# Second layer's mixing output taken tile by tile: first column chunk's halves in buffers of their own, the two chunks' order changed, the second tile's norm moved

## The reference, cut to what matters

```python
o = merge_branches(y_ml, y_ga, y_na, zg, w_branch[l], w_out[l])      # ... @ w_out
x = x + ga1 * rms_norm_2(o, g_post_mix[l])
f = conv_ffn(modulate(rms_norm_2(x, g_pre_ffn[l]), sh2, sc2), w_up[l], conv_w[l], conv_b[l], w_down[l])
x = x + ga2 * rms_norm_2(f, g_post_ffn[l])
```

## Time and profile before

| | |
|---|---|
| median of three runs | 1708.37 us |
| the profiled execution, its own time | 1708.59 us |
| its span in the profile | 1706.8 us |
| PE busy | 1670.8 us, 98% of the span |
| DVE busy | 1257.1 us, 74% |
| ACT busy | 842.5 us, 49% |

### The profile page before, as it was taken

One profiled execution on the slowest core, in us unless ns is written; L12 is line 12 of the kernel. 1 busy time (PEld: TensorE's weight loads), 2 busy tenths in 40 slices (PEclk: granted clock), 3 DMA queues, 4 the chain that ended last, 5 costly groups with the idle time before them and its releaser, 6 DMA issues.

```text
span 1706.8 us, 25221 instructions
## 1 busy us (share of the span) xinstructions
PE 1670.8 (98%) x9808; PEld 1426.8 (84%) x9808; DVE 1257.1 (74%) x2205; ACT 842.5 (49%) x1370; POOL 0.2 (0%) x4
## 2 busy tenths in 40 slices
PE   9989999999999999999999999999999999999998
PEld 9888888777787778888888888889778989979987
DVE  7999777875778798856877775347756786678864
ACT  6665555554334444347444442336553455466653
POOL 0000000000000000000000000000000000000000
PEclk9999999999999999999999999999999999999999
DMA  8646542231234335533545556324222444547553
GB/s 342 225 161 237 192 151 96 78 124 63 64 117 161 121 133 185 200 134 99 139 146 188 194 196 222 99 74 139 99 84 63 135 146 152 177 151 176 188 186 135
DMA packets 79078, 254.91 MB, mean 149 GB/s; under 512 B 14320, under 2 KB 18672, under 8 KB 78320
## 3 DMA queue, kind: packets, MB, share of 16 engines
q1 hardware_dynamic: 73488, 244.91, 42.9%
q10 hardware_dynamic: 5472, 8.39, 1.4%
HBM read 252.19 MB, written 1.07 MB: 148 GB/s over the span
## 4 chain that ended last, share of the span: by engine, by line
PE 76%; DVE 15%; ACT 5%; issue 3%; DMA 0%; ACTq 0%; SPq 0%; DVEq 0%
PE bank L725 64%; DVE w_lo L1828 4%; PE bank L868 2%; PE bank L1037 2%; PE bank L1023 2%; PE bank L1115 2%; PE bank L1014 2%; ACT w_hi L1225 1%; DVE mod_w L1885 1%; DVE probT L1885 1%; PE bank L1104 1%; DVE att L2455 1%; DVE xc L1928 1%; DVE resid_x L2321 0%; DVE bank L2453 0%
## 5 line engine op out<-in xcount | busy, mean ns | idle before, releaser
L1828 DVE TENSOR_TENSOR w_lo<-w_raw,w_hi 128x1024 fp32r<-128x1024 f32 (+1 forms) x356 | 427.2, 1211 | 253.8 <-ACT w_hi L1225 252.3
L1225 ACT ACTIVATE w_hi<-w_raw 128x1024 fp32r<-128x1024 f32 (+1 forms) x356 | 370.1, 1048 | 338.7 <-PE bank L725 284.8
L725 PE MATMUL bank<-hT_hi,w_hi 128*128 128x512 f32 (+1 forms) x1280 | 446.2, 349 | 1.7 <-ACT zo L1553 0.6
L725 PE MATMUL bank<-hT_hi,w_lo 128*128 128x512 f32 (+1 forms) x1280 | 437.8, 342 | 0.0
L725 PE MATMUL bank<-hT_lo,w_hi 128*128 128x512 f32 (+1 forms) x1280 | 437.6, 342 | 0.0
L725 PEld LDWEIGHTS bank<-hT_hi,w_hi 128*128 128x128 f32 x1280 | 241.7, 189 | 30.1 <-issue 3.1
L725 PEld LDWEIGHTS bank<-hT_hi,w_lo 128*128 128x128 f32 x1280 | 241.6, 189 | 28.0
L725 PEld LDWEIGHTS bank<-hT_lo,w_hi 128*128 128x128 f32 x1280 | 241.9, 189 | 27.1 <-issue 1.0
L1885 DVE SCALAR_TENSOR_TENSOR mod_w<-mod_w,c_rows 128x1024 f32<-128x1024 f32 x96 | 117.1, 1220 | 7.8 <-DMA mod_w<-in_mod_weights 7.8
L725 PE MATMUL bank<-w_hi,hT_hi 128*128 128x512 f32 x272 | 114.8, 422 | 0.4 <-issue 0.4
L725 PE MATMUL bank<-w_lo,hT_hi 128*128 128x512 f32 x272 | 106.6, 392 | 0.0
(11 more groups left out here) (393 smaller groups left out, 2796.8 us busy)
## 6 DMA issues: line engine op xcount, KB each, us to landing
w_raw<-in_weights SPq DMA_DIRECT2D x356, 512.0 KB, 4.0
mod_w<-in_mod_weights SPq DMA_DIRECT2D x96, 512.0 KB, 4.1
nbias<-in_window_bias ACTq DMA_DIRECT2D x32, 128.0 KB, 3.0
resid_c<-in_ctx ACTq DMA_DIRECT2D x2, 1024.0 KB, 6.1
gain_mix<-gain_rows SPq DMA_DIRECT2D x3, 512.0 KB, 5.6
gain_ffn<-gain_rows SPq DMA_DIRECT2D x3, 512.0 KB, 4.3
c_rows<-in_conditions SPq DMA_DIRECT2D x1, 1024.0 KB, 5.5
gatew<-in_gate_weights SPq DMA_DIRECT2D x1, 1024.0 KB, 11.5
```

The lines of the kernel that those rows point to most:

```text
L725: mm = pe.matmul(held[key][:, oc], st, mv_, start=(opens and k == 0 and t == 0 and i == 0), stop=(closes and k == tiles - 1 and t == 2), s ...
L1225: a.activation(w_hi[:, p % RING, :, used], w_raw[:, p % RING, :].rearrange("p (k n) -> p k n", k=KP)[:, :, used], ACT.Copy).then_inc(hi_re ...
L1828: v.tensor_tensor(w_lo[:, p % RING, :, used], w_raw[:, p % RING, :].rearrange("p (k n) -> p k n", k=KP)[:, :, used], w_hi[:, p % RING, :, ...
```

## The change

In the last layer only:

- The halves of A0 to A3 get places of their own (`hold_hi`, `hold_lo`), so their splits wait for no earlier piece; the waits of B0 to B3 and U0 to U3 on `piece_used` are renumbered to match.
- PE takes the mixing product in the order: A for tile 2, B for tile 2, B for tile 3, A for tile 3. The pieces of B are released by B for tile 3. `norm_T` of tile 2 stands behind the first piece of A for tile 3.
- `norm_T` of tile 3 stands behind the whole of tile 2's part of the first `w_up` chunk.
- ACT and DVE have programs of their own for this stage (`output_apart`, `post_apart`), with a small extra square root ahead of the first real one.

```diff
+HELD = stream().index(("w_out_2", LAYERS - 1, 0, 0))
...
+    hold_hi = sb("hold_hi", [P, RING, KP, COLS], R + 32 * KB, F32R)
+    hold_lo = [sb(f"hold_lo{i}", [P, 2, KP, COLS], (16 + 16 * i) * KB, F32R) for i in range(2)]
...
+    def used_before(p):
+        if HELD <= p < HELD + RING:
+            return 0
+        if HELD + RING <= p < HELD + 2 * RING:
+            return p - 2 * RING + 1
+        if HELD + 2 * RING <= p < HELD + 3 * RING:
+            return p - 2 * RING + 1
+        return p - RING + 1
...
+                turn_at = n if l == LAYERS - 1 and which == "ffn" else n - 1 if shared(l, which) or late else n // 2
...
-                        if gi == 0 and p == (n - 1 if shared(l, which) or late else n // 2):
+                        if gi == 0 and p == turn_at:
                             norm_T(l, which, 1)
...
+                    if gi == 0 and turn_at == n:
+                        norm_T(l, which, 1)
...
+                def out_apart():
+                    at = pieces[0]
+                    for c, t in ((0, 2), (1, 2), (1, 3), (0, 3)):
+                        key = (("wo", l, c), t - NT)
+                        ps = take(pe, key)
+                        for p in range(RING):
+                            i = at + RING * c + p
+                            if t == NT:
+                                pieces[0] = i + 1
+                                pe.wait_ge(hi_ready, i + 1)
+                                pe.wait_ge(lo_ready, i + 1)
+                                if c == 0:
+                                    pe.wait_ge(*merged_ready.at((l, KP * p + KP - 1)))
...
+                            if t > NT:
+                                mm.then_inc(piece_used, 1)
+                            if t > NT and c == 0 and p == 0:
+                                norm_T(l, "ffn", 0)
...
-                    if p >= RING:
-                        act.wait_ge(piece_used, p - RING + 1)
+                    if used_before(p) > 0:
+                        act.wait_ge(piece_used, used_before(p))
...
+            def output_apart(l):
...
+                split_hi(up)
+                act.wait_ge(*merged_ready.at((l, KD - 1)))
+                copied(0, 2, False)
+                a.activation(rs[:, 60:61], eps[:], ACT.Sqrt).then_inc(*A.next())
+                squared(1, 2, True)
+                rooted(2)
+                norm_root(*nxt, 2, o_of("mix", 2))
+                split_hi(up + 2)
+                copied(1, 3, False)
+                norm_hi(*nxt, 0, 0)
+                split_hi(up + 3)
+                norm_hi(*nxt, 0, 1)
+                split_hi(up + 4)
+                norm_hi(*nxt, 0, 2)
+                norm_hi(*nxt, 0, 3)
+                squared(0, 3, True)
+                rooted(3)
+                norm_root(*nxt, 3, o_of("mix", 3))
+                for p in range(KD // 2):
+                    norm_hi(*nxt, 1, p)
...
+            def post_apart(l, gains):
...
+                split_lo(up)
...
+                norm_gains(*nxt)
+                post_gains(*nxt)
+                gained(0, 2)
+                residual(1, 2)
+                norm_right(*nxt, 2)
+                split_lo(up + 2)
+                gained(1, 3)
+                norm_tmp(*nxt, 0, 0)
+                split_lo(up + 3)
+                norm_lo(*nxt, 0, 0)
+                norm_tmp(*nxt, 0, 1)
+                split_lo(up + 4)
+                norm_lo(*nxt, 0, 1)
+                norm_tmp(*nxt, 0, 2)
+                norm_lo(*nxt, 0, 2)
+                norm_tmp(*nxt, 0, 3)
+                norm_lo(*nxt, 0, 3)
+                residual(0, 3)
+                norm_right(*nxt, 3)
+                norm_second(*nxt)
```

More of the change, by code:

```diff
@@ L1170, in _ @@
                 merge(2)
-                for c in range(2):
+                def out_apart():
[11 more added lines that the diff above has]
+                                    pe.wait_ge(*merged_ready.at((l, KP * p + KP - 1)))
+                            hi, lo = halves_of(i)
+                            for kk in range(KP):
+                                k = KP * p + kk
+                                for j, (w, x) in enumerate(((hi, mg_hi), (hi, mg_lo), (lo, mg_hi))):
+                                    mm = pe.matmul(ps[:], tokens(x, k, slice(t * P, (t + 1) * P)), w[:, kk, :],
+                                                   start=(k == 0 and j == 0), stop=(k == KD - 1 and j == 2), skip_group_check=True)
+                            if t > NT:
+                                mm.then_inc(piece_used, 1)
+                            if t > NT and c == 0 and p == 0:
+                                norm_T(l, "ffn", 0)
+                        if t == NT:
+                            mm.then_inc(*filled(key))
+                        else:
+                            plan[("filled", key)] = ("piece", 0, at + (RING if c else 2 * RING), at + 2 * RING)
+                if last:
+                    out_apart()
+                for c in range(0 if last else 2):
                     gemm_tok(("wo", l, c), q_tts, mg_hi, mg_lo, by_bank=c == 1,
@@ L1175, in _ @@
                              inputs=None if c else lambda p, l=l: merged_ready.at((l, KP * p + KP - 1)))
-                if last:
-                    norm_T(l, "ffn", 0)
                 def turn_up():
@@ L1518, in output, with copied, squared, rooted @@
                                 act.dma_start(out[:, t - NT, :], resid[1][:, t - NT, :]).then_inc(out_stored, 16)
+            def output_apart(l):
+                nxt, up = (l, "ffn"), piece("w_up", l, 0)
+                def copied(c, t, end):
+                    key, o = (("wo", l, c), t - NT), o_of("mix", t)
+                    act.wait_ge(*filled_at(key))
+                    a.activation(o[:, c * COLS:(c + 1) * COLS], psum(key)[:], ACT.Copy).then_inc(*A.next())
+                    squared(c, t, end)
+                def squared(c, t, end):
+                    key = (("wo", l, c), t - NT)
+                    act.wait_ge(*filled_at(key))
+                    act.wait_ge(*A.last())
+                    a.activation(junk_of("mix", t), psum(key)[:], ACT.Square, accum_out=ss[:, 8 + 2 * t + c:9 + 2 * t + c])\
+                        .then_inc(*(A.tell(stat_ready, (l, "mix", t)) if end else A.drain(key)))
+                def rooted(t):
+                    act.wait_ge(*post_ms.at((l, "mix", t)))
+                    a.activation(rs[:, 4 + t:5 + t], ss[:, 24 + t:25 + t], ACT.Sqrt, scale=1.0 / D, bias=eps[:])\
+                        .then_inc(*A.tell(post_root, (l, "mix", t)))
+                split_hi(up)
[18 more added lines that the diff above has]
+                    norm_hi(*nxt, 1, p)
             for l in range(LAYERS):
@@ L2346, in post, with gained, residual @@
                         norm_second(*nxt)
+            def post_apart(l, gains):
+                nxt, up = (l, "ffn"), piece("w_up", l, 0)
+                def gained(c, t):
+                    key, o, cols = (("wo", l, c), t - NT), o_of("mix", t), slice(c * COLS, (c + 1) * COLS)
+                    dve.wait_ge(*drained_at(key))
+                    v.tensor_tensor(o[:, cols], o[:, cols], gains[:, 1, cols], ALU.mult).then_inc(*W.next())
+                def residual(c, t):
+                    key, o, cols = (("wo", l, c), t - NT), o_of("mix", t), slice(c * COLS, (c + 1) * COLS)
+                    dve.wait_ge(*stat_ready.at((l, "mix", t)))
+                    v.tensor_tensor(ss[:, 24 + t:25 + t], ss[:, 8 + 2 * t:9 + 2 * t], ss[:, 9 + 2 * t:10 + 2 * t], ALU.add)\
+                        .then_inc(*W.tell(post_ms, (l, "mix", t)))
+                    v.tensor_tensor(o[:, cols], psum(key)[:], gains[:, 1, cols], ALU.mult).then_inc(*W.drain(key))
+                    dve.wait_ge(*W.last())
+                    dve.wait_ge(*post_root.at((l, "mix", t)))
+                    v.reciprocal(ss[:, 28 + t:29 + t], rs[:, 4 + t:5 + t]).then_inc(*W.next())
+                    dve.wait_ge(*W.last())
+                    r = resid[1][:, t - NT, :]
+                    v.scalar_tensor_tensor(r, o, ss[:, 28 + t:29 + t], r, ALU.mult, ALU.add)\
+                        .then_inc(*W.tell(resid_ready, (*nxt, t)))
+                split_lo(up)
+                dve.wait_ge(gain_loaded, 16 * gain_loads(l, "mix"))
+                norm_gains(*nxt)
[18 more added lines that the diff above has]
+                norm_second(*nxt)
             for l in range(LAYERS):
```

22 lines of the change are left out of this document (17 added, 5 removed).

## The result

The changed kernel takes 1712.28 us, the median of ten runs (1711.97 to 1714.34); the kernel before takes 1708.13 us on the same chip (ten runs, 1707.83 to 1708.50). The ratio is 1.0025, with a 95% interval from 1.0016 to 1.0033: the change costs about 4.1 us.

What follows compares the result with a forecast made beforehand. PE, busy 98% of the span, was taken as the bound, so only its waits count; the chain moved the second `w_up` chunk from 1524.1 to 1527.0, +2.9 us, giving 1711.3 us, range 1708.6 to 1714.4.

Steps and rivals of the forecast that it cites:

- the forecast's own case: Second `w_up` chunk starts 2.9 us later through the ACT and DVE chain, giving 1711.3 us; chance 0.55.
- the clock rival: Half clock behind PE's 3.0 us idle at tile 3's diagonal: 1.4 us more, 1712.7 us; chance 0.30.
- The front: Mixing product up to tile 2's last bank: PE waits at A2 0.1, A3 0.9, B3 0.3; 1.3 us lost.
- Tile 2's statistics: Square of tile 2's last bank to ACT's turn to U0: 4.4 us, early table load saving 0.9.
- From U0 to tile 3's `norm_T`: ACT and DVE chain of splits, norm steps and tile 3's statistics: 18.95 us until tile 3's `norm_T` starts.
- Tile 3's part: From tile 3's `norm_T` to the second `w_up` chunk: 2.45 us until PE starts, then 5.56 us.
- The stage in all: From the first mixing matmul to the second `w_up` chunk's start: 2.9 us longer than before.
- The check by idle time: PE idle of 1.3, 1.5, 0.2, 3.0 and 0.65 us against 3.2 before, meant to confirm +2.9.
- the 4.4 us lost before: Kernel before, mixing product to second `w_up` chunk: 19.19 us against 14.8 for PE's work alone, restarts included.
- The splits of U2 and U3: Rival: made before the first modulation, they leave the chain, tile 3's diagonal comes 4.2 us earlier, 1707.1 us; chance 0.07.
- The starved ring: Rival: raw slots feed PE too slowly, B2 and B3 1.5 us late, 1712.8 us or more; chance 0.08.
- Slower by over 0.2%: Outcome measurably slower than the kernel before, above 1711.8 us; chance 0.50, against 0.47 same and 0.03 faster.

Runs made afterwards that it cites:

- front-mended kernel: Changed kernel with A1 split ahead of the last gates, A2 and A3 ahead of the last merged sums: 1711.16 us, ratio 1.0016.
- filled kernel: Changed kernel with 11 useless matmuls on PE ahead of the wait for tile 3's diagonal: 1711.81 us, run again 1711.92 us, ratio 1.0022 both times.
- all-mended kernel: Changed kernel with A1 to A3 split earlier, U0 to U3 splits moved and tile 2's norm steps overlapped on ACT and DVE: 1705.23 us, ratio 0.9981.
- old order mended: Kernel before the change, PE's order and buffers untouched, last layer's ACT and DVE programs reordered, extra root included: 1707.74 us, ratio 0.9995.

## Why the prediction was right, and where not

The forecast was 1711.3 us, the measured median is 1712.28, in the range; as a difference, +2.9 was forecast and +4.1 measured. About 3.2 of that is the forecast's own case, as the stage shows it. The rest, 0.9, is probably the clock rival, which came true in part of the executions; that share of the median is argued and not shown.

- **The front, 1.3 us.** The front-mended kernel puts it at 1.24 to 1.28. The forecast's parts are losses against a stream of matmuls 0.23 us apart, and so they have to be read from start to start: at A2 0.44 - 0.23 = 0.2 us (0.1 forecast), at A3 1.06 - 0.23 = 0.8 (0.9), at B3 0.2 (0.3), 1.25 in all. The idle that the timeline lists at A3 is less, 0.67. Tile 2's last bank released ACT 12.82 us after A0; 1495.6 - 1482.75 = 12.85 was forecast.
- **Tile 2's statistics, 4.4 us.** From the square to ACT's turn to U0, 1501.62 - 1497.20 = 4.42. The load moved early is worth 0.6 to 0.96 (0.9 forecast). The drain of about 1.38 us that the Trainium skill (ScalarE: Activation LUTs, What ACT_TABLE_LOAD costs) adds to a load isn't seen: the load took 1.28 us in the changed kernel too, and with the load back in the chain the norm came 0.96 us later, not the 0.96 + 1.38 = 2.3 of an estimate with that drain. Tile 2's `norm_T` waits for nothing, as forecast.
- **From U0 to tile 3's `norm_T`, 18.95 us.** Measured 1520.78 - 1501.62 = 19.16. The wait ahead of U1 was 1.70 (1.5), the one ahead of the diagonal 2.94 (3.0). That the chain runs through the places of the splits of U2 and U3 was shown by moving them: 1.75 us.
- **Tile 3's part, 2.45 + 5.56.** From `norm_T` to the second chunk 1528.90 - 1520.78 = 8.12 us. The stop behind the norm was 0.45 (0.65).
- **The stage in all.** 44.25 us forecast, 44.52 measured; +2.9 against +3.17. The difference of 0.3 is spread over the chain.
- **The check by idle time.** It doesn't come out as it stands: 1.3 + 1.5 + 0.2 + 3.0 + 0.65 = 6.65 against 3.2 makes 3.45, more than the 2.9 that it is to confirm, before any restart. It sets losses from start to start against idle as the trace lists it. Against the 4.4 us lost before, also from start to start, it gives 2.25 and some restarts. Measured, the stage's time without PE busy went from 41.35 - 38.14 = 3.21 to 44.52 - 38.66 = 5.86 us, 2.65 more. The sum itself doesn't use it.
- **The weakest step: the clock.** It stood as an alternative, all or nothing, with 1.4 us at a chance of 0.30, and the forecast's own number held none of it. It is neither: executions of one program differ. The price was too high as well: a fall costs 0.9 us in the stage. The whole difference between the two profiles of the changed kernel is 45.74 - 44.52 = 1.2, but 0.3 of it had come ahead of the norm (36.73 against 36.40). The excess of low-clock runs is 29/44 - 29/112 = 0.66 - 0.26 = 0.4. Two thirds of runs with low clock in place of a quarter can move a median across to the other group, and the filled kernel, at 3.1 and 3.4 us above the kernel before where the changed one is at 4.1 and 4.3, points the same way. Against it stand the overlapping intervals and the result's own five runs at high clock, 4.0 us up. So the clock stands in the stage of three profiled executions with its 0.9 us, and its share in the median's 0.9 stays open. The argument for 0.30, that 3.0 us lies nearer to the idle that fell (3.60) than to the one that didn't (1.80), took a length as if it decided. It doesn't, as the last section shows.
- **The rivals.** The splits of U2 and U3 didn't leave the chain by themselves. The edit that takes them from between the norm steps gives 1710.75 us and not the rival's 1707.1, because the rival was mis-sized: 4.2 us counted each split as gone, while it stands ahead of the steps instead and still takes its time there. In that execution a fall costs 0.9 us more. 1.75 us is what the move is worth; to win more, a split has to fill a wait, as in the all-mended kernel. The starved ring didn't come about. The load of B3 took 3.4 us. That of U0 took 5.3 instead of the 3.6 counted on, but it landed at 1496.0, 5.6 us before ACT came to it, and cost nothing.
- **The chances.** Slower by over 0.2% had 0.50. The ratio is 1.0025, its interval reaches down to 1.0016: just on that side.

The change's idea was sound and its ACT and DVE programs spent it. The order on PE gives 2.2 us (old order mended against all mended). Between the changed kernel and the mended one lie 44.52 - 38.10 = 6.4 us: 1.3 of them are the front, and the other 5.1 the placing of splits and norm steps, which no run takes fully apart.

## What to carry to other kernels

When PE's order is changed, the programs of the engines that feed it have to be written anew, from the chain that ends last: a split or copy of 1 us belongs where its engine would wait anyway, and a statistic stands ahead of everything that isn't needed sooner. Before work is moved, ask of each wait whether PE will merely arrive earlier at the same chain; a wait that keeps its length while all before it shrinks (2.94 us in three kernels) is a sign of it, and then what released PE last has to be found: here one step of DVE released PE and started the 4.57 us that PE then waited out. An idle stretch of PE of some 3 us behind such a chain is to be priced with a clock term in part of the runs (here 0.9 us in three of five profiled executions), not as yes or no.

## What the runs showed of the hardware

The clock's fall is not settled by how long PE was idle. The timeline of PE of the changed kernel has three long stretches ahead of the stage, in code that the kernel before shares:

```profile
93.86 0.46 PE L822 MATMUL bank<-v,sT 128*128 128x128 f32 x2 [3.61 <-issue]
```

```profile
124.94 0.44 PE L831 MATMUL bank<-tab,onrm 128*128 128x128 f32 x2 [2.37 <-DVE onrm L2089]
```

```profile
221.53 0.47 PE L956 MATMUL bank<-w_hi,mix_hi 128*128 128x512 f32 x1 [1.82 <-issue]
```

Behind 3.61 us idle the clock stayed at 1.00, behind 2.37 and 1.82 it fell to 0.50 for 3.4 us (windows above). In the kernel before it was the other way round: a fall behind 3.60, none behind 1.80, and none behind the middle stretch, which was 1.70 us there. All eleven profiled executions follow one of these two patterns. The first stretch is 3.60 or 3.61 us and the third 1.80 to 1.83 in every one of them. Six fell behind the first, had a middle stretch of 1.66 to 1.70, and fell behind neither of the others; five didn't fall behind the first, had a middle stretch of 2.37 to 2.40, and fell behind it and behind the third. A third case of this sort is the stage itself, where 2.94 us of idle brought a fall in three of five executions. The Trainium skill (TensorE: Matmul & The Clock Gate, Why this matters for your kernels) warns of idle gaps between bursts; the fall behind 3.60 us in the kernel before agrees with that, but by these rows neither does the longest gap always bring one (3.61) nor is the shortest safe (1.82). That the falls come from the gaps ahead of them is itself read from their place alone: the one at 126.40 begins 1.5 us after PE is back at work. What makes the difference between two executions of the same code I haven't found.
